# All weight chunks of a transformer block in fp32r high and low parts, and the modulation chunks moved behind attention's gates

## The chip, the core and the metric

One core of a Trainium2 chip runs the whole program as one launch. The metric is the device time in microseconds. Three runs of the kernel before took 2053.18, 2058.55 and 2112.91 us (median 2058.55 us).

## The reference, cut to what matters

Two blocks run one after the other on 256 tokens of 1024 channels. The first has two layers, and the change touches only these. Each layer is:

```python
h = rms_norm(x, norm_mix_pre[l])
proj = h @ w_in[l]            # q, k, v of three attentions, a small gate, conv and pooling inputs
...                           # compressed, selected and windowed attention; 31-tap conv; pooling
up = jnp.einsum("bsnc,ncd->bsnd", branches, w_branch[l])
gates = jax.nn.sigmoid((h @ w_gate[l]).reshape(bsz, seq, N_BRANCH, D_MODEL))
mix = jnp.einsum("bsnd,bsnd->bsd", gates, up) @ w_o[l]
x = x + rms_norm(mix, norm_mix_post[l])
hf = rms_norm(x, norm_ffn_pre[l])
u = causal_depthwise_conv(hf @ ffn_w_up[l], ffn_conv_w[l], ffn_conv_b[l])
gate, val = jnp.split(u, 2, axis=-1)
f = (jax.nn.gelu(gate, approximate=True) * val) @ ffn_w_down[l]
x = x + rms_norm(f, norm_ffn_post[l])
```

The second block (a state-space scan, attention and a mixture of experts) starts from six modulation vectors, `silu(c) @ w_mod + b_mod`. They don't depend on x. The kernel computes them inside the two layers of the first block, 24 steps of 128 columns in each layer, taken four at a time as six "mod steps".

## The kernel before, in words

**Weights come in chunks.** Every weight matrix is laid out in chunks of 128 partitions by 2048 float32 values, 1024 KB each, and TensorE works through them in one fixed order, 92 chunks in a layer. They pass through a ring of four slots, `ring`. SyncE loads chunk c + 4 into the slot of chunk c once TensorE has raised that slot's `used` semaphore (lines 398 to 402); the landed load raises the slot's `landed` semaphore. TensorE raises `used` of a chunk not at the chunk's last matmul but with the first matmul of the work behind it (`release` and `carry`, lines 419 to 428).

**Two forms of weights.** Some chunks are used as float32 straight from the ring: the projections (line 498), all `blocks_fm` chunks (line 526), the compression weights (line 555) and the modulation chunks (line 448). The others are split first, so that TensorE can use its fp32r form: ScalarE copies the chunk into a rounded high part (`split_hi`, line 386), VectorE subtracts that from the chunk and writes the low part (`split_lo`, line 392), and TensorE runs three matmuls, high by high, high by low and low by high. These are the branch projections (lines 717 to 721), `w_o` (736 to 740), the feed-forward's two matrices (759 to 763 and 777 to 781), and the experts of the second block. The activations of these matmuls are kept in two parts as well.

**Order of a layer's chunks:** two mod steps (4 chunks); key, value and query projections `kv`, `kv2`, `q`, `dq` (8 chunks); `c` and `ba` (2 + 2), four compression chunks, `bg` (2); 16 gate chunks with the four other mod steps laid between the first eight of them (a mod chunk, half a step, behind each); 12 branch and `w_o` chunks; 22 up and 11 down chunks of the feed-forward; one empty chunk.

**Orders of the engines.** Each engine executes its own instruction list strictly as it is written, and the lists are written by hand. What matters here is the attention stage. There are 12 attention items (kind, token tile t, head group g); items of t = 0 have 128 keys and those of t = 1 have 256. Turn i of the loop does on TensorE (lines 672 to 682): the scores of item i, one gate chunk with its mod chunk, the transposes of the probabilities of item i - 1 (`turn_probs`), and their product with the values (`values`, line 666). ScalarE's turn (lines 885 to 903): copy the gate result out of PSUM (`gate_out`), copy the mod row, copy the transposed probabilities of item i - 1 into `pt`, then the exponentials of item i. `values(i - 1)` waits for that `pt` copy. VectorE masks, takes maxima, normalizes, and runs ten steps of the 31-tap convolution in each turn. GpSimd has nothing to do in this stage. A fixed pool of PSUM regions is shared out by `Jobs`: a job claims its region when its last user is drained.

**The beginning of a layer:** ScalarE loads the column and row parameters (lines 801 and 802) and squares x; GpSimd takes the inverse root; VectorE waits for both parameter loads, scales x, and TensorE transposes it into `hT`. TensorE does the two early mod steps meanwhile.

Of the kernel before, what the change touches and what calls it, by code (L numbers as in the profile page):

```python
# [27 lines left out]
F32 = mybir.dt.float32  # L28
# [5 lines left out]
P = 128  # L34
T = 256
# [15 lines left out]
SPLITS = 3  # L51
FFN_CHUNKS = FB + FB // 2
# [5 lines left out]
def offsets(fields):  # L58
# [11 lines left out]
    ("w_ga", KD * 24),  # L70
])
ROWS, N_ROWS = offsets([("mix_post", D), ("ffn_post", D), ("sinks", 8)])
# [123 lines left out]
def plan_mods(jobs, steps):  # L196
    for i in steps:
        jobs.plan(("mod", i))
        if i - 1 in steps:
            jobs.plan(("modT", i - 1))  # L200


EARLY_MODS, MID_MODS = range(0, 2), range(2, MOD_STEPS)


def plan_layer(jobs):
    plan_mods(jobs, EARLY_MODS)
# [3 lines left out]
    jobs.plan(("modT", EARLY_MODS[-1]))  # L211
# [16 lines left out]
    for kv in range(2):  # L228
        jobs.plan(("hidT", kv), drains=2)
    jobs.plan(("bg", 1))  # L230
# [49 lines left out]
def layer_block(nc, l, mem, ring, landed, used, wts, psum, sems, cols_dram, rows_dram, loaded):  # L280
# [28 lines left out]
    lo_ready = sems("lo_ready")  # L309
# [9 lines left out]
    x, tm, hT, proj, gates, qTs, rkT = (mem[k] for k in ("x", "tm", "hT", "proj", "gates", "qTs", "rkT"))  # L319
# [3 lines left out]
    cdT = gates[:, 2048:3072].rearrange("p (m t) -> p m t", m=4)  # L323
    rtmp = gates[:, 3072:4480]
    rot = gates[:, 4480:7296].rearrange("p (t c) -> p t c", t=2)
    hfT, fT, split = (mem[k] for k in ("hfT", "fT", "split"))
# [2522 lines left out]
```

## Time and profile before

| what | us |
|---|---|
| runs of the kernel | 2053.18, 2058.55, 2112.91 |
| the profiled execution's own time | 2053.64 |
| its span in the trace | 2051.8 |
| layer 0 of the first block, about | 0 to 640 |
| layer 1, about | 640 to 1268 |
| TensorE busy | 1860.6 (91%) |
| VectorE busy | 953.2 (46%) |
| ScalarE busy | 647.4 (32%) |
| GpSimd busy | 217.5 (11%) |
| mean granted TensorE clock | 0.941 of full speed |

A time in the trace is counted from the start of the span. TensorE's busy time is that of overlapping matmuls, so the price of a chunk is read from start to start of the same instruction in two chunks, not from the mean duration of one. A float32 matmul stands in the trace as two matmul instructions, an fp32r one as one. An entry "x64" is 64 instructions of that line in a row; the bracket behind it says how long the engine stood idle before it and what ended the wait.

### The profile page before, as it was taken

The page shows a single profiled execution, that of the slowest core. Times are in us where ns is not written, and L with a number is a line of the kernel's source. Part 1 is how long each engine was busy: PE and PEld are TensorE (multiplying, and loading weights), DVE is VectorE, ACT ScalarE, POOL GpSimd, SP SyncE. Part 2 cuts the span into 40 slices and gives each one's busy share as a digit, 9 for nine tenths or more (in the row PEclk, how much of TensorE's full clock was granted, in tenths as well). Part 3 has the DMA queues.
Part 4 walks back from the last instruction along what each step waited for, and adds up shares of the span by engine and source line. Part 5 has one row for each costly group of instructions (what it writes and reads, how often), then busy time and mean ns, then how long its engine had stood idle before and what let it go on. Part 6 is the DMA issues. An engine that isn't in the chain of part 4 may idle for free. (4 is left out here: it accounts for less than half of the span.)

```text
span 2051.8 us, 24867 instructions
## 1 busy us (share of the span) xinstructions
PE 1860.6 (91%) x9940; PEld 1444.6 (70%) x9940; DVE 953.2 (46%) x1410; ACT 647.4 (32%) x987; POOL 217.5 (11%) x285
## 2 busy tenths in 40 slices
PE   6999998869996999998869997999899997899996
PEld 3577777869974477676859985544476645799995
DVE  1235464557742215454646743138434415355555
ACT  1122225445531112224545542111223401333331
POOL 0100000213310010000303320001520001000000
PEclk9999999989998999999989998899978997899998
DMA  7444422425455444522425545322110021355552
GB/s 275 143 185 164 185 84 102 152 106 182 180 182 219 163 184 145 204 85 80 154 97 182 185 168 188 123 82 82 41 42 1 1 103 62 106 183 189 179 183 82
DMA packets 39094, 279.81 MB, mean 136 GB/s; under 512 B 4432, under 2 KB 4688, under 8 KB 5840
## 3 DMA queue, kind: packets, MB, share of 16 engines
q1 hardware_dynamic: 37984, 272.44, 36.5%
q10 hardware_dynamic: 1008, 5.93, 0.8%
q8 instruction: 74, 1.21, 0.2%
q14 instruction: 28, 0.23, 0.0%
HBM read 277.30 MB, written 1.05 MB: 136 GB/s over the span
## 5 line engine op out<-in xcount | busy, mean ns | idle before, releaser
L526 PE MATMUL psum<-sb_hT,ring 128*128 128x256 f32 x1408 | 321.9, 388 | 2.2 <-DMA ring<-weights 2.1
L526 PEld LDWEIGHTS psum<-sb_hT,ring 128*128 128x128 f32 x1408 | 270.2, 194 | 49.1 <-issue 7.7
L392 DVE TENSOR_TENSOR sb_split<-ring,sb_split 128x2048 fp32r<-128x2048 f32 x90 | 212.4, 2360 | 123.7 <-ACT sb_split L386 123.4
L759 PE MATMUL psum<-sb_hfT,sb_split 128*128 128x256 f32 x704 | 201.4, 286 | 10.9 <-DVE sb_hfT L1279 10.9
L386 ACT ACTIVATE sb_split<-ring 128x2048 fp32r<-128x2048 f32 x90 | 171.9, 1910 | 114.9 <-PE psum L781 57.8
L762 PE MATMUL psum<-sb_hfT,sb_split 128*128 128x256 f32 x704 | 201.0, 286 | 0.0
L763 PE MATMUL psum<-sb_hfT,sb_split 128*128 128x256 f32 x704 | 200.9, 285 | 0.0
L1644 DVE TENSOR_TENSOR sb_split<-ring,sb_split 128x2048 fp32r<-128x2048 f32 x48 | 110.0, 2292 | 160.2 <-ACT sb_split L1639 160.2
L1937 PE MATMUL psum<-sb_hfS,sb_split 128*128 128x256 f32 x512 | 146.5, 286 | 2.5 <-PE psum L1959 2.1
L1940 PE MATMUL psum<-sb_hfS,sb_split 128*128 128x256 f32 x512 | 146.0, 285 | 0.0
L1941 PE MATMUL psum<-sb_hfS,sb_split 128*128 128x256 f32 x512 | 145.9, 285 | 0.0
L759 PEld LDWEIGHTS psum<-sb_hfT,sb_split 128*128 128x128 f32 x704 | 137.1, 195 | 11.4 <-DVE sb_hfT L1279 11.4
L762 PEld LDWEIGHTS psum<-sb_hfT,sb_split 128*128 128x128 f32 x704 | 137.1, 195 | 0.0
L763 PEld LDWEIGHTS psum<-sb_hfT,sb_split 128*128 128x128 f32 x704 | 137.0, 195 | 0.0
L1639 ACT ACTIVATE sb_split<-ring 128x2048 fp32r<-128x2048 f32 x48 | 91.6, 1908 | 95.8 <-PE psum L1898 47.0
L498 PE MATMUL psum<-ring,sb_hT 128*128 128x512 f32 x256 | 110.4, 593 | 0.0
L1937 PEld LDWEIGHTS psum<-sb_hfS,sb_split 128*128 128x128 f32 x512 | 99.4, 194 | 4.2 <-issue 3.8
L1309 DVE SCALAR_TENSOR_TENSOR sb_hq<-psum,sb_cols,sb_hq 128x254 f32<-128x254 f32 (+1 forms) x176 | 72.7, 475 | 61.8 <-ACT sb_hq L969 61.8
L1940 PEld LDWEIGHTS psum<-sb_hfS,sb_split 128*128 128x128 f32 x512 | 99.5, 194 | 0.3
L1941 PEld LDWEIGHTS psum<-sb_hfS,sb_split 128*128 128x128 f32 x512 | 99.4, 194 | 0.0
L1096 DVE SCALAR_TENSOR_TENSOR sb_acc<-sb_bglu,sb_cols,sb_acc 128x256 f32<-128x256 f32 x240 | 97.1, 476 | 0.0
L809 ACT ACTIVATE sb_gates<-psum 128x512 f32<-128x512 f32 x36 | 21.3, 597 | 232.7 <-PE psum L526 232.1
(352 smaller groups left out, 3221.2 us busy)
## 6 DMA issues: line engine op xcount, KB each, us to landing
ring<-weights SPq DMA_DIRECT2D x256, 1024.0 KB, 4.8
sb_rows<-rows ACTq DMA_DIRECT2D x2, 1028.0 KB, 10.6
sb_rows<-rows ACTq DMA_DIRECT2D x1, 2048.0 KB, 10.4
sb_cols<-cols ACTq DMA_DIRECT2D x2, 662.0 KB, 6.2
sb_x<-x_in SPq DMA_DIRECT2D x1, 1024.0 KB, 6.9
sb_y<-ctx_in SPq DMA_DIRECT2D x1, 1024.0 KB, 5.6
out<-sb_x SPq DMA_DIRECT2D x2, 512.0 KB, 2.7
sb_const<-const SPq DMA_DIRECT2D x1, 791.0 KB, 9.8
```

The costliest lines, as they stand in the source:

```text
L386: act.activation(slot[:, 0, :], ring[:, c % SLOTS, :], ACT.Copy).then_inc(hi_ready, 1)
L392: dve.tensor_tensor(slot[:, 1, :], ring[:, c % SLOTS, :], slot[:, 0, :].bitcast(F32), ALU.subtract).then_inc(lo_ready, 1)
L498: mm = pe.matmul(jobs.out((w, t)), hT[:, 4 * half + k, t * P:(t + 1) * P], chunk[:, k, :], start=(half == 0 and k == 0), stop=(half == 1 a ...
L526: mm = pe.matmul(jobs.out(name)[:, b * T:(b + 1) * T], chunk[:, k, b * P:(b + 1) * P], hT[:, k, :], start=(k == 0), stop=(k == KD - 1))
L759: mm = pe.matmul(out, hi[:, k, b * P:(b + 1) * P], hfT[:, 0, k, :], start=(k == 0), stop=False)
L762: pe.matmul(out, hi[:, k, b * P:(b + 1) * P], hfT[:, 1, k, :], start=False, stop=False)
L763: mm = pe.matmul(out, lo[:, k, b * P:(b + 1) * P], hfT[:, 0, k, :], start=False, stop=(k == KD - 1))
L1096: conv.up(dve.scalar_tensor_tensor(out=acc[:, b, :], in0=bglu[:, b, k:k + T], scalar=w, in1=acc[:, b, :], op0=ALU.mult, op1=ALU.add))
L1644: dve.tensor_tensor(split[:, n % SPLITS, 1, :], ring[:, (first_moe + n) % SLOTS, :], split[:, n % SPLITS, 0, :].bitcast(F32), ALU.subtract ...
L1937: mm = pe.matmul(out, hi[:, k, b * P:(b + 1) * P], hfS[:, 0, k, :], start=(k == 0), stop=False)
L1940: pe.matmul(out, hi[:, k, b * P:(b + 1) * P], hfS[:, 1, k, :], start=False, stop=False)
L1941: mm = pe.matmul(out, lo[:, k, b * P:(b + 1) * P], hfS[:, 0, k, :], start=False, stop=(k == KD - 1))
```

## The change

In each layer of the first block:

1. All weight chunks except the compression and modulation chunks are used in two parts: 30 more in a layer (8 projections, `c`, `ba`, `bg`, 16 gates). The normalized input is kept in two parts too (`hS`, in place of `hT`).
2. The low part is written where the chunk lay, in its ring slot (`ring_low` is the same memory as `ring`). High parts have two buffers up to the feed-forward (`HI_MIX`) and four in it (`HI_FFN`, before: three).
3. The low parts of gate chunks 0 to 12 are made by GpSimd, the others by VectorE.
4. All six mod steps lie behind the first twelve gate chunks; none is left at the start.
5. x and the constants are loaded ahead of the weights. The row parameters are loaded behind the projections, and those of the feed-forward later.
6. The small gate's product `ga` is computed turned round, four groups of 32 columns, and turned back by two matmuls.
7. The gates take other memory, and gate chunks run in the order of the branches that use them.

ScalarE's high parts are placed like this: those of the projections ahead of the copies of each pair; that of gate i + 2 right behind the copy of gate i.

```diff
+HI_MIX, HI_FFN = 2, 4
...
+MID_MODS = range(MOD_STEPS)
+
+def layer_chunks():
+    out = ["split"] * 12 + ["raw"] * 4 + ["split"] * 2
+    for i in range(16):
+        out.append("split")
+        if mid_mod_of(i) is not None:
+            out.append("raw")
+    return out + ["split"] * (12 + FFN_CHUNKS) + ["raw"]
+
+SPLIT_CHUNKS = [c for c, kind in enumerate(layer_chunks()) if kind == "split"]
+FIRST_C, FIRST_BA, FIRST_BG, FIRST_GATE, FIRST_UP, FIRST_WO, FIRST_FFN, FIRST_DOWN = 8, 10, 12, 14, 30, 38, 42, 64
+POOL_LOWS = range(FIRST_GATE, FIRST_GATE + 13)
...
     def split_hi(act, n):
 
-        c, slot, turns = split_slot(n)
-        if turns <= n < n_up or n >= n_up + turns:
-            act.wait_ge(used[(c - turns) % SLOTS], l * (N_LAYER_CHUNKS // SLOTS) + ((c - turns) // SLOTS + 1))
+        before = n - HI_MIX if n <= FIRST_FFN else n - HI_FFN if n >= FIRST_FFN + HI_FFN - 1 else -1
+        if before >= 0:
+            c = SPLIT_CHUNKS[before]
+            act.wait_ge(used[c % SLOTS], l * (N_LAYER_CHUNKS // SLOTS) + (c // SLOTS + 1))
+        c = SPLIT_CHUNKS[n]
         act.wait_ge(landed[c % SLOTS], (l * (N_LAYER_CHUNKS // SLOTS) + (c // SLOTS + 1)) * 16)
-        act.activation(slot[:, 0, :], ring[:, c % SLOTS, :], ACT.Copy).then_inc(hi_ready, 1)
+        act.activation(hi_of(n), ring[:, c % SLOTS, :], ACT.Copy).then_inc(hi_ready, 1)
...
@@ TensorE: one gate chunk in every turn @@
-                gate_chunks(i < len(ITEMS))
+                gate_chunks(1)
                 if i == 1:
                     cmp_out()
                 if i >= 1:
                     turn_probs(i - 1)
-                    gate_chunks(i in (3, 6))
                     values(i - 1)
             gate_chunks(16)
...
@@ ScalarE: gate_out @@
-                        copy_out(("gate", i), gates[:, i * 512:(i + 1) * 512])
+                        n = BRANCH_ORDER[i // 4]
+                        copy_out(("gate", i), gate_of[n][:, i % 4 * 512:(i % 4 + 1) * 512], func=ACT.Sigmoid if n == BRANCH_ORDER[-1] and i > 13 else ACT.Copy)
+                        split_hi(act, FIRST_GATE + i + 2)
                         if mid_mod_of(i) is not None and i % 2 == 1:
                             mods_out([mid_mod_of(i)])
...
@@ ScalarE, feed-forward loop @@
                 if j < FB:
-                    split_hi(act, n_up + j + SPLITS)
+                    split_hi(act, FIRST_FFN + j + HI_FFN)
...
@@ VectorE, behind the attention loop @@
+            split_lo(dve, FIRST_GATE + 13)
             out_low(len(ITEMS) - 1)
-            split_lo(dve, 0)
             conv_steps(4 * TAPS)
+            for n in range(FIRST_GATE + 14, FIRST_UP + 1):
+                split_lo(dve, n)
...
@@ GpSimd @@
+            for n in POOL_LOWS:
+                split_lo(pool, n)
+                pool.wait_ge(lo_pool, low_count(n))
...
@@ SyncE, start of the program @@
                     sp.dma_start(mem["cond"][:, :], cond).then_inc(conditioned, 16)
+                    sp.dma_start(mem["x"][:, :, :], x_in.rearrange("(t p) d -> p t d", p=P)).then_inc(loaded, 16)
+                    sp.dma_start(mem["const"][:, :], const).then_inc(placed, 16)
                     for s in range(SLOTS):
                         sp.dma_start(ring[:, s, :], weights[s]).then_inc(landed[s], 16)
```

## Rows read from the trace of the kernel before

**Rows 1.** The page, part 1: busy time and share of the span

```profile
PE 1860.6 (91%) x9940; PEld 1444.6 (70%) x9940; DVE 953.2 (46%) x1410; ACT 647.4 (32%) x987; POOL 217.5 (11%) x285
```

**Rows 2.** TensorE timeline, one turn: start, busy, instruction, count, [idle before]

```profile
192.88 1.06 PE L448 MATMUL psum<-ring,sb_cvec 128*32 128x512 f32 x8
...
195.24 1.07 PE L666 MATMUL psum<-sb_pt,sb_proj 128*64 128x512 f32 x2 [0.70 <-ACT sb_pt L809]
...
197.33 7.17 PE L526 MATMUL psum<-sb_hT,ring 128*128 128x256 f32 x32
...
204.43 1.06 PE L448 MATMUL psum<-ring,sb_cvec 128*32 128x512 f32 x8
```

**Rows 3.** Timeline of ScalarE, the same turn

```profile
194.10 0.60 ACT L809 ACTIVATE sb_mrow<-psum 128x512 f32<-128x512 f32 x1 [0.51 <-PE psum L448]
...
194.59 0.59 ACT L809 ACTIVATE sb_pt<-psum 128x512 f32<-128x512 f32 x1
```

**Rows 4.** Timeline of the load queue, the same turn

```profile
194.21 0.86 SPq L402 DMA_DIRECT2D ring<-weights  x2
```

**Rows 5.** Source view of the loads, line 402, 150 to 240 us

```profile
DMA to landing us min/median/max: 4.7/5.7/8.0
```

**Rows 6.** Timeline of TensorE, a turn with 256 keys

```profile
282.53 1.93 PE L666 MATMUL psum<-sb_pt,sb_proj 128*64 128x512 f32 x4
...
284.39 1.99 PE L640 MATMUL psum<-sb_rkT,sb_qTs 64*128 64x256 f32 x8
```

**Rows 7.** Timeline of ScalarE, the same turn

```profile
281.30 0.59 ACT L809 ACTIVATE sb_pt<-psum 128x512 f32<-128x512 f32 x1
...
282.64 0.60 ACT L809 ACTIVATE sb_pt<-psum 128x512 f32<-128x512 f32 x1 [0.75 <-PE psum L435]
```

**Rows 8.** Timeline of TensorE, weights as whole float32

```profile
31.02 55.18 PE L498 MATMUL psum<-ring,sb_hT 128*128 128x512 f32 x128
...
90.43 13.98 PE L526 MATMUL psum<-sb_hT,ring 128*128 128x256 f32 x64
```

**Rows 9.** Timeline of ScalarE, one chunk to the next, both part forms

```profile
458.34 1.02 ACT L969 ACTIVATE sb_hq<-psum,sb_cols 128x256 f32<-128x256 f32 x2 [1.21 <-PE psum L763]
...
464.10 1.02 ACT L969 ACTIVATE sb_hq<-psum,sb_cols 128x256 f32<-128x256 f32 x2 [2.63 <-PE psum L763]
...
592.63 1.92 ACT L386 ACTIVATE sb_split<-ring 128x2048 fp32r<-128x2048 f32 x1 [3.52 <-PE psum L781]
...
598.07 1.92 ACT L386 ACTIVATE sb_split<-ring 128x2048 fp32r<-128x2048 f32 x1 [3.52 <-PE psum L781]
```

**Rows 10.** Timeline of VectorE, one low part

```profile
573.02 2.29 DVE L392 TENSOR_TENSOR sb_split<-ring,sb_split 128x2048 fp32r<-128x2048 f32 x1 [2.54 <-ACT sb_split L386]
```

**Rows 11.** Source view of GpSimd line 2586: ns least, median, most

```profile
L2586 POOL TENSOR_TENSOR sb_wx<-sb_xs,sb_sm x6: 1899/1900/2236, 1457.3 to 1474.7; 128x1024 f32<-128x1024 f32 x6
```

**Rows 12.** Windows: busy PE, PEld, DVE, ACT, POOL; granted clock, DMA share, GB/s

```profile
322.60:325.10 2.50, 0.01 (x1) 0.00 (x0) 1.56 (x3) 0.84 (x4) 0.00 (x0) 1.00 0.32 134
...
327.30:330.50 3.20, 3.20 (x4) 0.54 (x3) 0.00 (x0) 0.49 (x1) 0.00 (x0) 0.50 0.00 0
```

**Rows 13.** Timeline of TensorE, first and last gate of layer 0

```profile
153.04 8.83 PE L526 MATMUL psum<-sb_hT,ring 128*128 128x256 f32 x32
...
330.65 7.17 PE L526 MATMUL psum<-sb_hT,ring 128*128 128x256 f32 x32
```

**Rows 14.** Timeline of TensorE between the projections and attention, layer 0

```profile
125.42 1.68 PE L555 MATMUL psum<-ring,sb_gates 128*32 128x256 f32 x16 [2.94 <-DMA ring<-weights]
...
127.90 9.46 PE L526 MATMUL psum<-sb_hT,ring 128*128 128x256 f32 x32 [0.81 <-DMA ring<-weights]
```

**Rows 15.** Timeline of VectorE, start of layer 1

```profile
653.30 1.42 DVE L992 TENSOR_SCALAR sb_tm<-sb_x,sb_small 128x1024 f32<-128x1024 f32 x2 [13.24 <-DMA sb_rows<-rows]
```

**Rows 16.** Timeline of TensorE, first projection of layer 1

```profile
658.60 41.88 PE L498 MATMUL psum<-ring,sb_hT 128*128 128x512 f32 x97
```

**Rows 17.** The page, part 5: busy, mean ns | idle before, what ended it

```profile
L777 PE MATMUL psum<-sb_split,sb_fT 128*128 128x512 f32 x176 | 70.0, 398 | 5.6 <-DVE sb_hq L1309 5.6
```

More of the change, by code:

```diff
@@ L193, in mid_turn_of, with low_count @@
     return MID_MODS[i // 2 - 1] if i % 2 == 0 and 1 <= i // 2 <= len(MID_MODS) else None
[L196 to L203, printed above, removed]
+MID_MODS = range(MOD_STEPS)
[9 more added lines that the diff above has]
+POOL_LOWS = range(FIRST_GATE, FIRST_GATE + 13)
+def low_count(n):
+    return sum((m in POOL_LOWS) == (n in POOL_LOWS) for m in range(n + 1))
 def plan_layer(jobs):
-    plan_mods(jobs, EARLY_MODS)
     for c in range(2):
@@ L277, with layer_block @@
 BRANCH_ORDER = (2, 0, 3, 1)
-def layer_block(nc, l, mem, ring, landed, used, wts, psum, sems, cols_dram, rows_dram, loaded):
+def layer_block(nc, l, mem, ring, ring_low, landed, used, wts, psum, sems, cols_dram, rows_dram, loaded, placed):
     filled = {r: sems(f"filled_{r}") for r in REGION}
@@ L511, in _ @@
             jobs.claim(pe, "ga")
[L512 removed]
+            for part in range(2):
                 for k in range(KD):
[L514 to L516 removed]
+                    mm = pe.matmul(jobs.out("ga")[32 * (k % 4):32 * (k % 4) + 32, 0:T], C("w_ga", 32 * k, 32 * k + 32),
+                                   hS[:, part, k, :].bitcast(F32), start=(part == 0 and k < 4), stop=(part == 1 and k >= 4))
+                    if part == 0 and k == 0:
                         carry(mm)
@@ L572, in _ @@
                 jobs.fill(mm, ("hidT", kv))
+            jobs.wait_drained(pe, "ga")
+            jobs.claim(pe, "gaT")
+            for t in range(TT):
+                mm = pe.matmul(jobs.out("gaT")[:, 24 * t:24 * t + 24], gaT[:, t * P:(t + 1) * P], K("sel", 0, 24), start=True, stop=True)
+            jobs.fill(mm, "gaT")
             release(blocks_fm(("bg", 1)))
@@ L726, in _ @@
                 for half in range(2):
-                    hi, lo = (part.rearrange("p (k n) -> p k n", k=4) for part in next_split(8 + 2 * c + half))
+                    hi, lo = (part.rearrange("p (k n) -> p k n", k=4) for part in next_split())
                     for i in range(2):
@@ L1231, in _ @@
                     jobs.wait_filled(dve, name)
-                    g2 = gates[:, n * 2048 + i * 512:n * 2048 + (i + 1) * 512]
+                    g2 = gate_of[n][:, i * 512:(i + 1) * 512]
+                    if n == BRANCH_ORDER[-1] and i >= 2:
+                        jobs.wait_drained(dve, ("gate", 12 + i))
                     if bi == 0:
@@ L1254, in _, with residual @@
                                   ALU.subtract).then_inc(mix_lo, 1)
-            for n in range(9, n_up):
+            for n in range(FIRST_WO + 1, FIRST_FFN + 1):
                 split_lo(dve, n)
-            def residual(kind, g, first):
+            def residual(kind, first):
                 for t in range(TT):
@@ L2652, in place @@
                     mem1[k] = stack.enter_context(nc.sbuf_tensor(f"sb_{k}", [P, *s], dtype))
+            place(first, MEM_HI)
             with ExitStack() as phase:
@@ L2656, in build_program @@
             place(first, MEM_BR1)
+            with ExitStack() as phase:
+                place(phase, MEM_ROT)
             with ExitStack() as phase:
@@ L2661, in build_program @@
                 place(phase, MEM_UP)
-            for fields, dtype in ((MEM_FFN_SPLIT, F32R), (MEM_FFN, F32)):
-                for k, s in fields.items():
-                    mem1[k] = first.enter_context(nc.sbuf_tensor(f"sb_{k}", [P, *s], dtype))
+            place(first, MEM_FFN)
             with nc.Block() as block:
@@ L2700, in build_program @@
             with nc.Fori(0, LAYERS) as l:
-                layer_block(nc, l, mem1, ring, landed, used, weights, psum, sems, cols, rows, loaded)
+                layer_block(nc, l, mem1, ring, ring_low, landed, used, weights, psum, sems, cols, rows, loaded, placed)
                 nums = [s.num for s in layer_sems]
```

351 lines of the change are left out of this document (188 added, 163 removed).

## The prediction

> **What bounds the kernel now.** The page first: TensorE is busy for 91% of the span and no other engine for half of it [rows 1]. So a microsecond off TensorE's list is worth one, unless another engine's list then ends later. Next the TensorE timeline over one turn of layer 0's attention [rows 2]. From the mod chunk at 192.88 to the next at 204.43 are 11.55 us, 7.10 of them the gate chunk, and only 0.70 idle, waiting for ScalarE's copy of the probabilities. ScalarE has made that copy by 195.18 because nothing stands before it in its list but two short copies [rows 3]. Last the load queue: the slots of the gate chunk and the mod chunk just used are refilled from 194.21 on, 1.33 us after 192.88 [rows 4], and a load lands 4.7 us after its issue at the least, 5.7 in the median [rows 5]. Today the next chunk but one can't be wanted before 204.43, where TensorE leaves the gate between; the load is hidden. The change alters exactly this.
>
> **What TensorE gains.** A float32 chunk costs 55.18 / 8 = 6.90 us with 512 columns and 13.98 / 2 = 6.99 us with 256 [rows 8]. In parts the same chunk takes 598.07 - 592.63 = 5.44 us (24 matmuls of 512) and 464.10 - 458.34 = 5.76 us (48 of 256) [rows 9], 0.120 us for each of the latter. Per layer: 8 projections x 1.46 = 11.7 us; c and ba 4 x 1.23 = 4.9; the turned small gate about 1.6 (32 narrow matmuls in four column groups, nearest the compression chunks' form in [rows 14]: 1.68 us for 16 with the clock low). The Trainium skill, TensorE: Matmul & The Clock Gate, "Wait — 56ns, not 53.3ns?", gives the start-to-start time as columns by clock plus 2.5 ns, so 0.109 us at 256. By that a chunk would take 5.24 us and the 44 chunks of this width in both layers 23 us less than in my sum; the trace's 0.120 us is the measurement and I keep it.
>
> **Feeding the projections** costs nothing in a steady stream: from a chunk's release, 1.92 us for the high part and 2.29 for the low [rows 9, 10] and about 0.3 between them are 4.5, less than 5.44. The cover is thin (0.9 us). Between c and ba it tears: ScalarE puts a high part before the copies that free PSUM regions for ba, which I price at one high part, 2.0. At the compression chunks TensorE already waits 2.94 and 0.81 us for loads [rows 14]; now bg waits for high and low part behind the landing, +4.4, against two cheaper chunks (-2.5) and some small work (-0.4): +1.5. One more high part stands before the rotated queries' copies: +1.2. Projections to the first gate, per layer: -11.7 - 4.9 - 1.6 + 2.0 + 1.5 + 1.2 = -13.5; two layers -27.0.
>
> **The attention turn.** ScalarE now makes the high part of gate i + 2 directly behind the copy of gate i. In a layer the gates and mod chunks alternate up to gate 11, two chunks in a turn, four slots: chunk gate i + 2 goes into the very slot that gate i has just left. So ScalarE waits for a whole load. Queued behind it are the mod row's copy, the pt copy and the exponentials; `values(i - 1)` waits for the pt copy, and behind `values` on TensorE stand the next scores and the next gate. From the start of the mod chunk: 1.33 to the issue [rows 4], 4.7 to landing [rows 5], 1.91 high part, 0.60 pt copy [rows 3], 0.06, then 2.09 from `values` to the next gate's start [rows 2], 5.76 for the gate. That is 16.45 us against 11.55. The mod chunk, its turning and the transposes hide in the wait. A turn with an odd gate copies a mod row first, +0.5 [rows 3].
>
> **The clock.** In this turn TensorE idles some 5 to 6 us. In [rows 12] an idle stretch of 2.5 us is followed by 3.2 us at half the granted clock (1.2 for 2.4 GHz) while TensorE is busy all the time: 1.6 us lost. I charge 1.6 for each such wait; 0 and, from the same row stretched over the values, scores and gate of the turn, 7.85 are the ends.
>
> **The stage added up,** from the first gate's start. Gate 0: 5.76 + 1.6 = 7.4. To the end of gate 1, no probabilities yet: 7.85. Gate 2, behind the compressed attention's copy, which also waits: 6.03 + 1.91 + 0.5 + 0.6 + 5.76 + 1.6 = 16.4. Gates 3 to 6: 4 x (16.45 + 1.6) + 1.0 = 73.2. Gates 7 and 8, scores over 256 keys (+0.85, 1.99 against 1.16 to 1.2) [rows 6]: 38.3. Gates 9 to 11, also a second transpose and copy (+1.34 [rows 7]) and longer values (+0.86 [rows 6]): 3 x 21.1 + 0.5 = 63.8. Gate 12, whose successor's load is no longer late: 16.3. Gate 13 waits for a low part that VectorE makes only behind the last weighing: 18.0. Gates 14 and 15, again behind VectorE's low parts: 23.3. Sum 264.5 us. Today it is from 153.04 to 337.66, 184.6 us [rows 13]. So +79.9 a layer, +159.8 in all.
>
> GpSimd's low parts cost nothing here: 1.90 us for 1024 columns [rows 11] make 3.8 for 2048, bounded by 1.9 (a fixed cost only) and 7.6 (twice, beside a busy VectorE), and each has a turn of 16 us and a gate's lead. Their cover would last even at the old pitch of 11.55. VectorE's and ScalarE's added work in the turns (1.91 us of ScalarE) lies in waits.
>
> **The rest.** At the program's start x and the constants land earlier, and row parameters hold nobody; the first projection moves from 31.0 to about 19, behind a chain of about 7.2 us from the scaled x (three scalings, parts, then one low part of 2.29): -12.0. In layer 1 VectorE no longer waits for rows until 653.30 [rows 15] but starts at 650, so the two high-low chains take what was saved and the projection starts at 658.5 as now [rows 16], on a low clock: +1.6. In the feed-forward four high buffers make the same pattern, chunk j + 4 waits for the slot of chunk j, but it only delays ScalarE by 2 us in a turn of 5.76 and TensorE leads on; at its end TensorE waits longer for the last drain, today 5.6 / 2 = 2.8 us [rows 17], by 3.6 to 5: +8.0 in all, between 0 and 10. The second buffer filled earlier ahead of the branches: -2.8. The row and feed-forward parameter loads are three queue entries on ScalarE of some 0.5 us each, in waits.
>
> **Sum:** 2053.6 (the profiled execution's own time) - 27.0 + 159.8 - 12.0 + 1.6 + 8.0 - 2.8 = 2181.2, so 2181 us. That execution is 5 us below the median shown, 2058.55.
>
> **Rivals.** (1) *The load is no wait*, the forecast's opposite: if ScalarE found the chunk landed, the turn would be TensorE's alone. It decides at a landing within about 1.7 us of the release, where TensorE's own mod chunk and transposes end. Then the stage gives 32 x 1.23 = -39.4 and pays 11.8 for four more mod halves and two turnings per layer: 2053.6 - 27.0 - 39.4 + 11.8 - 12.0 + 1.6 + 8.0 - 2.8 = 1994. For it: TensorE idles little now and the copy waits of 0.7 are small. Against it: no load in the stretch landed in under 4.7 us, and the slot arithmetic leaves no lead. A misreading of mine somewhere in the order is what I give it its chance for: 0.13. (2) *The clock stays low* from one turn to the next, as each gate is followed by a longer idle time than any gate has now: 11 turns x 6.25 x 2 = +137, 2318 us: 0.04. For it: both idle stretches of [rows 14] together had a gate chunk at 9.46. Against: in [rows 13] 8.83 us is the worst that a low clock did to one gate without them. (3) *Half the wait*: TensorE or the queue has a lead of 3 us that I don't see; 22 turns x 3.0 and half of the clock's price are -66 - 22: 2093, around the 2% line, 0.07. The forecast has 0.76. The Trainium skill, DMA: Bandwidth & Descriptors, "Rules for kernel authors", says to issue a load early and wait late; the change waits as early as it can, and the 4.7 us row is why that would hurt.
>
> **Range and chances.** Within the forecast: without the clock's price (28 waits x 1.6) 2136, with landing at the median of 5.7 in all 22 waits 2203, with the clock's price doubled 2226, both together 2248. To reach 8 in 10 the range goes down through the half wait: 2085 to 2245. I count as no change what lies within 2% (41 us), about what a measurement of this kernel can tell. Faster 0.13; same 0.06; slower 0.81.
>
> **What would show it.** In the changed kernel's trace ScalarE's high-part line must stand under "DMA ring<-weights" as releaser for over 100 us in total (11 waits of about 5.4 in each layer), and the TensorE line of the values product must show idle time behind ScalarE's pt copy of 4 to 6 us a turn in place of 0.7. Start to start of gate chunks 16 to 22 us; projections 5.44 a chunk; first projection near 19 us; granted clock below 0.90 in the attention windows. The prediction is wrong if the pitch of turns stays under 12 us, if the pt copy isn't what `values` waits for, or if the high parts wait for GpSimd's or VectorE's low parts instead of the load.

## The result, and the profile after

The changed kernel takes 2240.47 us, the median of 4 runs (2239.11 to 2243.20); the kernel before, on the same chip, 2059.22 (4 runs). One of those four, 2112.91 us, fell into a slower state of the chip, and the ratio leaves it out: 1.089, 95% interval 1.087 to 1.092, so 181 us or 9% slower. I had forecast 2181 us in a range of 2085 to 2245: the direction and the mechanism are right, the size is 59 us short, and the measured time lies 5 us inside the top of the range.

The profiled execution spans 2237.3 us where before it was 2051.8. Its page, parts 1, 2 and 5 (the columns are those of [rows 1, 17]):

```profile
PE 1869.7 (84%) x10780; PEld 1507.6 (67%) x10780; DVE 1047.0 (47%) x1452; ACT 754.9 (34%) x1055; POOL 382.2 (17%) x311
...
PEclk9987778898999898777889899979987999789998
...
L404 ACT ACTIVATE sb_hi<-ring 128x2048 fp32r<-128x2048 f32 x118 | 225.7, 1912 | 404.2 <-DMA ring<-weights 251.8
...
L410 POOL TENSOR_TENSOR ring_low<-ring,sb_hi 128x2048 fp32r<-128x2048 f32 x26 | 119.9, 4610 | 426.0 <-ACT sb_hi L404 426.0
```

TensorE falls from 91% to 84% of a longer span, and its clock stands at 0.7 or 0.8 through both attention stages (slices 3 to 8 and 16 to 21 of 55.9 us). ScalarE's high part waits 251.8 us for loads; 58.1 of them, in 11 waits, lie in layer 0's stage of gates and as many in layer 1's, the others at loads elsewhere. Who waits for ScalarE shows in the waits of TensorE (total us, times, longest):

```profile
PE psum L690 <- ACT sb_pt L822: 78.8, 12, 7.5
...
PE psum L454 <- ACT sb_pt L822: 52.1, 12, 7.5
...
PE psum L454 <- ACT sb_cpT L822: 15.0, 2, 7.5
```

`values` and the second transposes waited 0.7 us a turn [rows 2]; now it is up to 7.5, and 145.9 us in all with the compressed attention's copy. One turn of layer 0, which answers to [rows 2]; the timeline of TensorE (start, duration, line, idle time before it and what ended it):

```profile
194.66 1.07 PE L467 MATMUL psum<-ring,sb_cvec 128*32 128x512 f32 x8
195.65 0.65 PE L454 MATMUL psum<-sb_const,sb_sc 128*128 128x128 f32 x4
203.60 1.97 PE L690 MATMUL psum<-sb_pt,sb_proj 128*64 128x512 f32 x2 [7.29 <-ACT sb_pt L822]
205.50 2.07 PE L664 MATMUL psum<-sb_rkT,sb_qTs 64*128 64x128 f32 x8
207.50 0.58 PE L545 MATMUL psum<-sb_hS,sb_hi 128*128 128x256 f32 x1
```

ScalarE in the same turn, answering to [rows 3]:

```profile
194.76 0.60 ACT L822 ACTIVATE sb_tm<-psum 128x512 f32<-128x512 f32 x1 [10.33 <-PE psum L549]
200.67 1.91 ACT L404 ACTIVATE sb_hi<-ring 128x2048 fp32r<-128x2048 f32 x1 [5.31 <-DMA ring<-weights]
202.48 0.58 ACT L822 ACTIVATE sb_mrow<-psum 128x512 f32<-128x512 f32 x1
202.96 0.59 ACT L822 ACTIVATE sb_pt<-psum 128x512 f32<-128x512 f32 x1
```

and the load queue, answering to [rows 4]:

```profile
195.98 0.86 SPq L421 DMA_DIRECT2D ring<-weights  x2
```

So: modulation chunk at 194.66, issue 1.32 us later, landed 4.69 after that, high part 1.91, mod row, pt copy, and `values` at 203.60. What follows runs at half clock. The same turn in windows (us; busy us and count of each engine; granted clock; share and GB/s of the DMA engines):

```profile
196.30:200.30 4.00, 0.01 (x1) 0.00 (x0) 0.00 (x0) 0.00 (x0) 0.00 (x0) 1.00 0.79 295
...
202.00:203.60 1.60, 0.00 (x0) 0.00 (x0) 0.00 (x0) 1.60 (x4) 0.88 (x1) 0.50 0.33 138
203.60:207.50 3.90, 3.90 (x10) 2.06 (x10) 0.00 (x0) 1.48 (x8) 3.63 (x1) 0.50 0.01 4
207.50:211.80 4.30, 4.30 (x21) 4.30 (x21) 4.02 (x10) 0.00 (x0) 0.00 (x0) 0.51 0.00 0
211.80:215.20 3.40, 3.40 (x30) 3.29 (x28) 2.26 (x6) 0.00 (x0) 0.00 (x0) 1.00 0.00 0
```

Where the 185.5 us of the span lie, from the starts of TensorE's groups in both traces (layer 0 / layer 1):

| stretch | before | after | measured | forecast |
|---|---|---|---|---|
| start to the first projection | 31.0 | 20.2 | -10.8 | -12.0 |
| eight projections | 55.0 / 55.0 | 46.5 / 47.1 | -16.4 | -23.4 |
| small gate to gate 0 | 67.0 / 67.2 | 75.1 / 75.7 | +16.6 | -3.6 |
| gate 0 to the end of gate 15 | 184.6 / 184.6 | 280.4 / 280.6 | +191.8 | +159.8 |
| branches and output projection | 92.4 / 92.3 | 90.9 / 90.7 | -3.1 | -2.8 |
| feed-forward | 200.6 / 203.5 | 205.2 / 204.7 | +5.9 | +8.0 |
| change of layers | 27.9 | 27.5 | -0.5 | +1.6 |
| the rest | 790.5 | 792.6 | +2.1 | 0 |
| sum | | | +185.6 | +127.6 |

Two stretches hold 52 of the 58 us between measured and forecast: 32 us in attention, 20 us ahead of it. The rest is the second block, which no edit here touches. From the same matmul of that block to the end the twelve traces take 699.3 to 703.6 us, so a difference of 4 us between two times can lie there; where a few microseconds matter, the experiments below are read by stretches.

### The profile page after: what moved, and what is told of

Its sections match the earlier page's. It is cut to its first block and busy times, and to the rows that moved or that the text cites. A ratio compares the mean times of both kernels' runs of the same rounds, so it can differ in the third digit from the quotient of the medians.

```text
span 2237.3 us, 26793 instructions
## 1 busy us (share of the span) xinstructions
PE 1869.7 (84%) x10780; PEld 1507.6 (67%) x10780; DVE 1047.0 (47%) x1452; ACT 754.9 (34%) x1055; POOL 382.2 (17%) x311
## 5 line engine op out<-in xcount | busy, mean ns | idle before, releaser
L404 ACT ACTIVATE sb_hi<-ring 128x2048 fp32r<-128x2048 f32 x118 | 225.7, 1912 | 404.2 <-DMA ring<-weights 251.8
L410 DVE TENSOR_TENSOR ring_low<-ring,sb_hi 128x2048 fp32r<-128x2048 f32 x92 | 211.7, 2303 | 231.6 <-ACT sb_hi L404 231.6
L545 PE MATMUL psum<-sb_hS,sb_hi 128*128 128x256 f32 x704 | 225.0, 320 | 40.3 <-DVE ring_low L410 25.2
L548 PE MATMUL psum<-sb_hS,sb_hi 128*128 128x256 f32 x704 | 218.6, 310 | 0.0
L549 PE MATMUL psum<-sb_hS,ring_low 128*128 128x256 f32 x704 | 216.9, 308 | 0.0
L777 PE MATMUL psum<-sb_hfT,ring_low 128*128 128x256 f32 x704 | 198.0, 281 | 0.0
L545 PEld LDWEIGHTS psum<-sb_hS,sb_hi 128*128 128x128 f32 x704 | 155.8, 221 | 55.5 <-DVE ring_low L410 32.1
L1701 DVE TENSOR_TENSOR sb_split<-ring,sb_split 128x2048 fp32r<-128x2048 f32 x48 | 110.0, 2292 | 160.1 <-ACT sb_split L1696 160.1
L548 PEld LDWEIGHTS psum<-sb_hS,sb_hi 128*128 128x128 f32 x704 | 155.6, 221 | 0.0
L549 PEld LDWEIGHTS psum<-sb_hS,ring_low 128*128 128x128 f32 x704 | 155.5, 221 | 0.0
L1696 ACT ACTIVATE sb_split<-ring 128x2048 fp32r<-128x2048 f32 x48 | 91.6, 1908 | 94.3 <-PE psum L1955 47.0
L1994 PEld LDWEIGHTS psum<-sb_hfS,sb_split 128*128 128x128 f32 x512 | 99.2, 194 | 4.1 <-issue 3.8
```

Source lines behind the costliest of these rows:

```text
L404: act.activation(hi_of(n), ring[:, c % SLOTS, :], ACT.Copy).then_inc(hi_ready, 1)
L410: eng.tensor_tensor(low_of(n), ring[:, SPLIT_CHUNKS[n] % SLOTS, :], hi_of(n).bitcast(F32), ALU.subtract)\
L545: mm = pe.matmul(out, hi[:, k, bs], hS[:, 0, k, :], start=(k == 0), stop=False)
L548: pe.matmul(out, hi[:, k, bs], hS[:, 1, k, :], start=False, stop=False)
L549: mm = pe.matmul(out, lo[:, k, bs], hS[:, 0, k, :], start=False, stop=(k == KD - 1))
L777: mm = pe.matmul(out, lo[:, k, b * P:(b + 1) * P], hfT[:, 0, k, :], start=False, stop=(k == KD - 1))
```

## Experiments

**1. The high part behind the exponentials** (changed kernel, one step moved):

```diff
+            later = []
+
+            def late_parts():
+                while later:
+                    split_hi(act, later.pop(0))
...
-                        split_hi(act, FIRST_GATE + i + 2)
+                        later.append(FIRST_GATE + i + 2)
...
                 if i < len(ITEMS):
                     exps(i)
+                late_parts()
```

> The changed kernel, with one thing moved: in the attention loop ScalarE makes the high part of gate i + 2 behind the exponentials of the turn, not directly behind the copy of gate i. The same work, the same loads, the same two high buffers. Theory of the prediction (ScalarE's wait for a whole load stands in front of the pt copy): nothing of the turn is queued behind that wait any more, TensorE sets the turn again at 10 to 10.6 us (11.55 before, less 1.3 for the gate chunk in parts), the stage from the first gate to the end of gate 15 falls from 280.6 us to 170 to 180, and the time from 2240 to about 2030 (2015 to 2050). Rival A (the loss comes from the modulation chunks in every turn, or from GpSimd's low parts, and not from where ScalarE waits): the stage stays above 250 us, the time above 2180. Rival B (half of it each): 2100 to 2150.

Measured: 2067.15 us (9 runs), ratio to before 1.006 (1.0044 to 1.0076). 173 of the 181 us are gone. The even turns are 10.3 us (gate chunks at 203.59 and 213.88 in layer 0), and the pt copy is waited for by 0.70 us again. ScalarE still waits for loads, 246.6 us in the whole program for 337.0 (both kinds of high part counted) and 13.1 for 58.1 in layer 0's stage, but with nothing behind the wait that TensorE wants in that turn. The stage is 197.5 us, not 170 to 180, and the time lies 37 us above what I expected and outside the range of 2015 to 2050. TensorE's and ScalarE's timelines, then VectorE's and GpSimd's:

```profile
180.86 0.58 PE L545 MATMUL psum<-sb_hS,sb_hi 128*128 128x256 f32 x1 [5.68 <-POOL ring_low L410]
...
203.59 0.38 PE L545 MATMUL psum<-sb_hS,sb_hi 128*128 128x256 f32 x1
...
211.79 1.07 PE L690 MATMUL psum<-sb_pt,sb_proj 128*64 128x512 f32 x2 [0.70 <-ACT sb_pt L822]
...
213.88 0.38 PE L545 MATMUL psum<-sb_hS,sb_hi 128*128 128x256 f32 x1
...
215.62 1.92 ACT L404 ACTIVATE sb_hi<-ring 128x2048 fp32r<-128x2048 f32 x1 [2.26 <-DMA ring<-weights]
...
206.69 8.38 DVE L1165 SCALAR_TENSOR_TENSOR sb_acc<-sb_bglu,sb_cols,sb_acc 128x256 f32<-128x256 f32 x10
...
206.50 4.73 POOL L410 TENSOR_TENSOR ring_low<-ring,sb_hi 128x2048 fp32r<-128x2048 f32 x1 [5.85 <-ACT sb_hi L404]
```

Gates 2 and 3 wait 2.7 and 5.7 us for GpSimd's low part, gates 13 and 14 wait 4.8 and 4.0 for VectorE's. And ten filter steps of VectorE, 4.04 us elsewhere, last 8.38 beside a low part of 4.73. The wait behind the gate's copy is shown as the cause; a second cost comes up, on GpSimd.

**2. The high part between pt copies and exponentials** (against experiment 1):

```diff
+                late_parts()
                 if i < len(ITEMS):
                     exps(i)
-                late_parts()
```

> As late_hi, but the high part of gate i + 2 stands between the pt copies and the exponentials of the turn. ScalarE still waits for the load in mid turn, only the waiter differs: values no longer hang on it, the exponentials do. Worked out for the turns over 128 keys: 1.3 + 4.7 + 1.9 from the modulation chunk's start to the high part's end, 1.6 for four exponentials, 1.1 for the weighing make 10.6 us, where TensorE comes to the next transposes after 11.3: covered. Over 256 keys about 2.0 and 1.8: 11.7, 0.4 to 1 us a turn short in five turns. Theory of the prediction (what costs is values behind the pt copy): 2030 to 2050, at most 20 us behind late_hi. Rival (any wait of ScalarE for a load within the turn costs about its length): above 2130.

Measured: 2095.35 us (4 runs), ratio 1.017 (1.011 to 1.024), 28 us behind experiment 1: neither the 20 of the theory nor the rival's 2130. VectorE, GpSimd and TensorE in a turn:

```profile
198.26 2.96 DVE L1237 TENSOR_TENSOR sb_small<-sb_small 128x4 f32<-128x4 f32 x1
...
196.62 4.57 POOL L410 TENSOR_TENSOR ring_low<-ring,sb_hi 128x2048 fp32r<-128x2048 f32 x1 [11.45 <-ACT sb_hi L404]
...
202.00 1.00 PE L454 MATMUL psum<-sb_const,sb_sc 128*128 128x128 f32 x4 [1.22 <-DVE sb_sc L1240]
```

A product over four columns, 0.16 us elsewhere, lasts 2.96 and ends with GpSimd's low part at 201.2. The weighing is late by that, TensorE waits 1.22 us, and the next gate begins on half clock (8.06 us for 5.92). That the late weighing comes from GpSimd is so far read from the times alone; experiment 10 tests it.

**3. TensorE kept busy in the wait** (transposes repeated; the waits stay):

```diff
+WARM = 10
...
-                    mm = pe.transpose(out[0:n, i * P:(i + 1) * P], b, ident)
+                    mm = pe.transpose(out[0:n, i % 4 * P:(i % 4 + 1) * P], b, ident)
...
-                    transpose4(("PT", a, t, g, kb), [sc[:, i % 2, j, kb * P:(kb + 1) * P] for j in range(4)])
+                    blocks = [sc[:, i % 2, j, kb * P:(kb + 1) * P] for j in range(4)]
+                    transpose4(("PT", a, t, g, kb), blocks * (WARM if kb == 0 and i < 11 else 1))
```

> The changed kernel with the waits left in and TensorE kept busy in them: the four transposes of the probabilities are made ten times over (about 6 us in a wait of 6 to 7.4 us), in the 11 turns whose gate is followed by a load. The outputs are the same. What the granted clock costs is measured by this. Theory 1 (the forecast's price of 1.6 us for each wait): 22 waits give back 35, 2205. Theory 2 (read from the changed kernel's trace: values, scores and the first 4.3 us of the gate run at half clock after each wait, 0.9 + 0.9 + 2.1 = 3.9 us): turns fall from 20.7 to about 16.8 us, 22 of them give back 84, about 2155 (2140 to 2175). Theory 3 (the slow matmuls are not the clock, or repeated transposes don't keep it): 2240 to 2245.

Measured: 2219.13 us (4 runs), ratio 1.081 (1.075 to 1.086): above theory 1's 2205 and below theory 3's 2240, so none of the three came out. A transpose at full clock takes 0.116 us, so the filling was too short. The windows from the end of a wait of 3.57 us on, and from the end of the next, 2.10 us:

```profile
199.64:202.36 2.72, 2.72 (x11) 1.69 (x11) 0.00 (x0) 1.47 (x8) 2.72 (x1) 0.75 0.00 0
202.36:207.00 4.64, 4.64 (x22) 4.64 (x22) 4.36 (x11) 0.00 (x0) 0.91 (x1) 0.50 0.00 0
...
219.22:221.30 2.08, 2.08 (x10) 1.16 (x10) 0.00 (x0) 1.48 (x8) 2.08 (x1) 1.00 0.00 0
221.30:227.10 5.80, 5.80 (x49) 5.72 (x48) 5.41 (x14) 0.00 (x0) 2.08 (x1) 1.00 0.00 0
```

The clock held behind waits of 1.19 and 2.10 us and fell behind those of 3.57 and 3.47, but in this trace it fell behind one of 2.31 as well (0.67 from 258.06 to 260.90, then 0.50). The expectation of experiment 4 calls the first of these 4.5 us, with the last transposes counted in, and leaves out the wait of 2.31.

**4. The same with the wait filled:**

```diff
-WARM = 10
+WARM = 13
...
-                    transpose4(("PT", a, t, g, kb), blocks * (WARM if kb == 0 and i < 11 else 1))
+                    transpose4(("PT", a, t, g, kb), blocks * (WARM + 3 * (i % 2) if kb == 0 and i < 11 else 1))
```

> As warm_turns, with more of the repeated transposes: sixteen times where no row of modulations is turned, thirteen times where one is. At full clock a transpose took 0.116 us, so ten rounds filled only 4.6 us and left gaps of 2.1 to 4.5 us; in that kernel the clock held over gaps of 1.2 and 2.1 us and fell in those of 3.5 and 4.5. Now 7.4 and 6.0 us are filled. Theory (the granted clock falls only where TensorE stands idle, and the low clock adds 3.5 to 4 us to a turn over 128 keys and about 1.5 to one over 256 keys): all gates of these turns take 5.9 us, turns come every 16.6 to 17.3 us, 6 or 7 turns of 3.6 and 4 of 1.5 us in each layer give back 60 us: 2175 to 2190. Rival (the clock falls for another reason): near 2219, as warm_turns.

Measured: 2190.64 us (4 runs), ratio 1.066 (1.062 to 1.069), 0.6 us above the theory's range of 2175 to 2190. The windows from the product with the values on:

```profile
202.00:204.10 2.10, 2.06 (x10) 1.16 (x10) 0.00 (x0) 1.52 (x8) 2.10 (x1) 1.00 0.00 0
204.10:208.00 3.90, 3.90 (x33) 3.87 (x33) 3.59 (x9) 0.00 (x0) 1.62 (x1) 1.00 0.02 4
```

Gates 3 to 7 start at 187.24, 204.13, 220.56, 237.48 and 254.79: every 16.4 to 17.3 us, against 20.3 to 21.9 in the changed kernel. From gate 2 to gate 11 it is 161.6 us against 190.9: the half clock costs 29.3 us over nine turns, 3.3 a turn: 3.8 to 4.7 in the six from gate 3 to gate 9, 1.5 to 1.7 in the other three. The repeated transposes cost 7 us a layer in the two last turns that have them, where no load is late. So of 59 us some 45 are left, which is what the two layers are shorter by; the other 3.5 of the 48.8 us between the two spans lie in the second block.

**5. The low parts of gates 0 and 1 on VectorE:**

```diff
-POOL_LOWS = range(FIRST_GATE, FIRST_GATE + 13)
+POOL_LOWS = range(FIRST_GATE + 2, FIRST_GATE + 13)
...
+            split_lo(dve, FIRST_GATE)
...
                     cmp_weigh()
+                    split_lo(dve, FIRST_GATE + 1)
```

> The changed kernel with the low parts of gates 0 and 1 on VectorE in place of GpSimd. In the changed kernel's trace VectorE's gating product ahead of gate 0 lasts 3.27 us and the first four filter steps 5.59 us where they took 0.69 and 1.37 before, and both lie beside a low part on GpSimd. Theory (the two engines get in each other's way): 0.69 and 1.37 us again, the first gate starts about 3.5 to 4.5 us earlier in each layer, the time falls by 6 to 9 us. Rival (the length comes from somewhere else, such as the data's place): the durations stay, VectorE has 4.6 us more in its list and the time rises by 0 to 5 us.

Measured: 2225.20 us (4 runs), ratio 1.083 (1.079 to 1.087), 15 us faster than the changed kernel (14.1 by the spans) where I expected 6 to 9. The low part of gate 0 now stands ahead of bg's gating product. VectorE, GpSimd and gate 0 in the changed kernel:

```profile
121.66 3.27 DVE L1139 TENSOR_TENSOR sb_bglu<-sb_bglu,sb_sc 128x512 f32<-128x512 f32 x1 [2.28 <-ACT sb_sc L822]
132.13 5.59 DVE L1154 TENSOR_SCALAR sb_acc<-sb_bglu,sb_cols 128x256 f32<-128x256 f32 x4
...
119.86 4.53 POOL L410 TENSOR_TENSOR ring_low<-ring,sb_hi 128x2048 fp32r<-128x2048 f32 x1 [36.57 <-ACT sb_hi L404]
132.95 4.62 POOL L410 TENSOR_TENSOR ring_low<-ring,sb_hi 128x2048 fp32r<-128x2048 f32 x1 [8.57 <-ACT sb_hi L404]
...
141.82 0.55 PE L545 MATMUL psum<-sb_hS,sb_hi 128*128 128x256 f32 x1 [3.69 <-DVE sb_brS L1174]
```

and with the low parts moved:

```profile
121.65 0.68 DVE L1140 TENSOR_TENSOR sb_bglu<-sb_bglu,sb_sc 128x512 f32<-128x512 f32 x1
...
131.76 1.37 DVE L1155 TENSOR_SCALAR sb_acc<-sb_bglu,sb_cols 128x256 f32<-128x256 f32 x4
...
137.69 0.38 PE L545 MATMUL psum<-sb_hS,sb_hi 128*128 128x256 f32 x1
```

The durations are again those of before. Gate 0 starts 4.1 us earlier with no wait, and at full clock (its first matmul 0.38 us, not 0.55), so it also ends 2.2 sooner; I had left the clock out of this expectation too. That the two engines hold each other up is said by the Trainium skill too, SBUF — State Buffer, "Who interferes with whom": a VectorE instruction with both inputs in SBUF, or in a two-port mode, and a GpSimd instruction that reads SBUF lock each other out for a whole instruction. The trace agrees for two inputs, with 3.27 for 0.69 us and 2.96 for 0.16. The third, 5.59 for 1.37, has one input tensor; whether it ran in a two-port mode the trace doesn't show. It is the rule that I should have weighed against "GpSimd's low parts cost nothing here".

**6. The feed-forward's high part one step later:**

```diff
                 if j >= 1:
+                    split_hi(act, FIRST_FFN + j - 1 + HI_FFN)
...
-                if j < FB:
-                    split_hi(act, FIRST_FFN + j + HI_FFN)
```

> The changed kernel with the feed-forward's high part of chunk j + 3 made behind the first filter step of j, in place of chunk j + 4 behind the activation of j - 1, and VectorE's low part one step later too. TensorE waits 6.8 and 5.6 us ahead of the down projection in the changed kernel, where it waited 2.8 before. Theory of the prediction (ScalarE's wait for the slot just left delays the last drains): the wait goes back to about 2.8 or less and the time falls by 7 to 10 us, 2231. Rival (it is the GpSimd product, 1.65 us a chunk where it took 0.82, that is late): the wait stays at 5 us or more.

Measured: 2233.20 us (4 runs), ratio 1.086 (1.083 to 1.089), 7.3 us faster than the changed kernel (6.7 by the spans). The down projection's first matmul in the changed kernel and in this one:

```profile
655.11 0.77 PE L791 MATMUL psum<-sb_hi_ffn,sb_fT 128*128 128x512 f32 x1 [6.79 <-issue]
```

```profile
651.45 0.47 PE L791 MATMUL psum<-sb_hi_ffn,sb_fT 128*128 128x512 f32 x1 [2.85 <-issue]
```

2.8 us, as before [rows 17]. The rival falls too: GpSimd's product became slower still, 2.48 us in the mean for 1.65, and the long wait is gone all the same. The page, part 5:

```profile
L1450 POOL TENSOR_TENSOR sb_cpad<-sb_hq 128x256 f32<-128x256 f32 x44 | 109.1, 2480 | 135.6 <-ACT sb_hq L1007 135.6
```

**7. The modulation chunks alone** (kernel before, float32 chunks; with them comes the change's one gate chunk in every turn):

```diff
-EARLY_MODS, MID_MODS = range(0, 2), range(2, MOD_STEPS)
+EARLY_MODS, MID_MODS = range(0, 0), range(MOD_STEPS)
...
-                gate_chunks(i < len(ITEMS))
+                gate_chunks(1)
...
-                    gate_chunks(i in (3, 6))
...
-                turned = {1: 0, 3: 1, 4: 2, 6: 3}
+                turned = {1: 0, 3: 1, 5: 2, 7: 3, 9: 4, 11: 5}
```

> The kernel before with one part of the change alone: all six modulation steps of a layer stand behind gate chunks (one half behind each of gates 0 to 11), none ahead of the projections; chunks stay float32, x and the row parameters are loaded as before. Theory of the prediction (the loss needs a high part that waits for the slot just left; a float32 chunk is wanted only a whole turn later): no more than the moved work itself, 2 steps of 3 us a layer moved from where they were partly hidden, 2050 to 2068. Rival A (the alternation of gates and modulation chunks in every turn costs by itself): 20 us or more above before, over 2077.

Measured: 2052.00 us (10 runs), ratio 0.9977 (0.9956 to 0.9999), within the 2050 to 2068 expected. Its TensorE, one turn:

```profile
202.97 7.17 PE L523 MATMUL psum<-sb_hT,ring 128*128 128x256 f32 x32
...
212.43 1.07 PE L663 MATMUL psum<-sb_pt,sb_proj 128*64 128x512 f32 x2 [0.71 <-ACT sb_pt L805]
...
214.52 1.78 PE L523 MATMUL psum<-sb_hT,ring 128*128 128x256 f32 x7
```

11.55 us, 0.71 idle, as in [rows 2]. Gates and modulation chunks in turn, with the same slots, cost 1.8 us of the stage (186.5 for 184.6). The loss needs the high part in ScalarE's list. The first projection starts at 23.3 us here: 7.7 of the 10.8 us won at the start are there as soon as the modulation chunks have left it; what loading x first would give by itself no run shows.

**8. The orders mended together** (experiments 1, 5 and 6; gate 3's high part ahead of gate 2's copy; bg's sigmoid ahead of gate 0's high part; low parts of gates 13 to 15 on GpSimd):

```diff
-POOL_LOWS = range(FIRST_GATE, FIRST_GATE + 13)
+POOL_LOWS = range(FIRST_GATE + 2, FIRST_GATE + 16)
...
-            split_hi(act, FIRST_GATE)
             copy_out(("bg", 0), sg[:, 0, :], func=ACT.Sigmoid)
+            split_hi(act, FIRST_GATE)
```

> The changed kernel with the four orders mended together: high parts of gates behind the exponentials (as late_hi; that of gate 3 ahead of gate 2's copy), low parts of gates 0 and 1 on VectorE and those of gates 13 to 15 on GpSimd, bg's sigmoid ahead of gate 0's high part, the feed-forward's order of ffn_order. From late_hi's 2067: gates 0 and 1 -15 (as front_low), sigmoid -3, feed-forward -9, the waits of 4.8 and 4.0 us ahead of gates 13 and 14 -17, half of those ahead of gates 2 and 3 -8: about 2015 (2005 to 2035), 1 to 2.5% faster than before. Rival (something else is late in their place, above all GpSimd with 4.6 us for each low part): 2045 to 2065.

Measured: 2009.52 us (5 runs), ratio 0.977 (0.975 to 0.979), as expected (2005 to 2035). Gates 13 and 14 no longer wait; gate 2 still does, 2.4 us for GpSimd.

**9. All low parts on VectorE:**

```diff
-POOL_LOWS = range(FIRST_GATE + 2, FIRST_GATE + 16)
+POOL_LOWS = range(0)
...
                 if i >= 1:
                     weigh(i - 1)
+                    split_lo(dve, FIRST_GATE + (2 if i == 1 else i + 2))
```

> As all_mended, with every low part on VectorE and none on GpSimd: 2.29 us in place of 4.6 each, that of gate i + 2 behind the weighing of turn i. Theory (a low part on GpSimd costs twice: 4.6 us until TensorE may start, and VectorE's instructions with two inputs in memory held up beside it): gate 2's wait of 2.4 us and the half clock behind it go (3.7), four waits of 0.7 us for the weighing too (2.8), both in each layer: 2009.5 - 13, about 1997 (1990 to 2005). Rival (VectorE becomes what sets the turn: 3.4 for mask and weighing, 2.3 low part, 4.0 filter, 0.2 are 9.9 us of the 10.3 to 11.2 that TensorE takes, and more over 256 keys): 2010 to 2030.

Measured: 1988.32 us (5 runs), ratio 0.967 (0.966 to 0.969): 69 us or 3.3% faster than before, 252 faster than the changed kernel, with the same arithmetic, and 9 us below what I expected, just under the range of 1990 to 2005. Page and waits of TensorE:

```profile
PE 1777.1 (89%) x10780; PEld 1443.9 (73%) x10780; DVE 1089.6 (55%) x1478; ACT 756.4 (38%) x1055; POOL 298.8 (15%) x285
...
PE psum L454 <- ACT sb_pt L822: 8.4, 12, 0.7
PE psum L690 <- ACT sb_pt L822: 7.1, 10, 0.8
```

Of the 145.9 us of waits behind ScalarE's copies about 17 are left (0.74 a layer for the compressed attention's copy); the first gate to the end of gate 15 is 166.7 us (137.21 to 303.90). VectorE's low part takes 2.28 us and the ten filter steps behind it 4.05:

```profile
189.29 2.28 DVE L410 TENSOR_TENSOR ring_low<-ring,sb_hi 128x2048 fp32r<-128x2048 f32 x1
191.49 4.05 DVE L1167 SCALAR_TENSOR_TENSOR sb_acc<-sb_bglu,sb_cols,sb_acc 128x256 f32<-128x256 f32 x10
```

**10. Experiment 9 with the high part ahead of the exponentials:**

```diff
+                late_parts()
                 if i < len(ITEMS):
                     exps(i)
-                late_parts()
```

> As all_vector, with the high part of gate i + 2 between the pt copies and the exponentials, as in mid_hi. mid_hi was 28 us slower than late_hi where I expected at most 20, and in its trace a product over 4 columns on VectorE lasted 2.96 us (0.16 elsewhere) beside a low part on GpSimd; the weighing came late and TensorE's clock fell. Theory (the shortfall of mid_hi beyond what its wait costs comes from GpSimd): without GpSimd's low parts 2 to 15 us above all_vector. Rival (it is ScalarE's wait in mid turn itself, GpSimd only happens to be there): again 25 to 40 us above all_vector.

Measured: 2000.73 us (5 runs), ratio 0.973 (0.971 to 0.974), 12.4 us above experiment 9, within the theory's 2 to 15, where with GpSimd's low parts it was 28.2. The traces of layer 0 show where each lies. From gate 3 to gate 12 this kernel takes 107.9 us and experiment 9 the same; with GpSimd's low parts it was 124.7 in experiment 2 against 113.0 in experiment 1. So in these turns ScalarE's wait costs nothing by itself, and what it cost came through GpSimd. What is left comes from one place in each layer: ScalarE's wait in turn 0 makes the first exponentials late, the weighing and VectorE's low part of gate 2 behind them too, and gate 2 waits 1.82 us and takes 8.66 in place of 5.92. From gate 0 to gate 3 are 32.9 us for 27.5, which makes 10.7 us in two layers; the other 3.9 of the 14.6 us between the two spans lie in the second block. (Between the pairs lie the other orders of experiment 8 too; the low parts of gates 13 to 15 and the feed-forward are outside these turns.)

```profile
154.16 0.58 PE L545 MATMUL psum<-sb_hS,sb_hi 128*128 128x256 f32 x1 [1.82 <-DVE ring_low L410]
```

## Why the prediction was right in kind and short in size

**The attention turn: right, nearly to the tenth.** The forecast chained 1.33 + 4.7 + 1.91 + 0.60 + 0.06 + 2.09 + 5.76 = 16.45 us, 16.95 with a mod row. With the clock held up (experiment 4) turns come every 16.43 and 16.89 to 16.92. Taking that one wait out of the way of the pt copy gives back 173 us (experiment 1). The stage by gates, from the end of the gate before to the end of its own, layer 0: gate 0 8.1 (forecast 7.4), gate 1 7.9 (7.85), gate 2 16.6 (16.4), gates 3 to 6 81.9 (73.2), 7 and 8 43.9 (38.3), 9 to 11 63.3 (63.8), 12 15.9 (16.3), 13 19.2 (18.0), 14 and 15 23.7 (23.3). Gates 3 to 8 hold 14.3 of the 15.9 us by which the stage is longer than forecast.

**The clock's price: the step that failed.** "I charge 1.6 for each such wait; 0 and ... 7.85 are the ends." Measured 3.3 a turn, 3.8 to 4.7 from gate 3 to gate 9. The 1.6 came from a stretch [rows 12] in which TensorE was at work again as the clock fell. Here the clock is at half already at 202.0, the wait ends at 203.6, and values, scores and the first 4.3 us of the gate lie in it; all dense matmuls, which take twice the time. The bound of 7.85 was right, the choice near its lower end was not: a stretch behind a wait of 7.3 us was read from one behind a wait of 2.5. That is 15 us a layer. In three of the nine turns (from gate 2, 9 and 10 on) the charge was right, 1.5 to 1.7 us.

**GpSimd's low parts "cost nothing here": the second step that failed.** The duration, 4.6 us, lay between the bounds (1.9 and 7.6), 0.8 above my 3.8. In the changed kernel's own turns it hides, as the wait is longer. Ahead of gate 0 it holds up VectorE (experiment 5: 15 us in both layers with the clock that follows), and once the turns are short it is the next wait (experiments 1, 8 and 9). "Their cover would last even at the old pitch" held from gate 4 on, where no gate waits for a low part in experiment 1 until gate 13, and not for gates 2 and 3, which wait 2.7 and 5.7 us.

**Small gate to gate 0: -1.8 a layer forecast, +8.3 measured.** The stall between c and ba is 1.5 us (2.0 forecast). From ba to bg are 24.0 us for 22.1, as forecast (4.4 for the longer wait, 2.5 off for ba's two chunks). Left out was what ScalarE's high part of gate 0 stands in front of: bg's sigmoid, for which the second bg chunk waits 3.9 us. With the sigmoid first it waits 2.1 (experiment 8), and on low clock the chunk takes 8.0 us. The rest is VectorE, above.

**Projections: -8.2 a layer, forecast -11.7.** At full clock a chunk takes 24 x 0.232 = 5.6, not 5.44, and the first matmuls behind a wait of 5.5 us run at half clock, about 2 us. The Trainium skill's start-to-start time (TensorE: Matmul & The Clock Gate, "Wait — 56ns, not 53.3ns?"), by which I weighed 5.24 us for a chunk over 256 columns, isn't reached here: from gate 1's start to the next instruction are 5.85 us at full clock. Keeping the trace's 5.76 was right.

**The feed-forward's end** waits 6.8 and 5.6 us for 2.8, forecast 3.6 to 5 us more; experiment 6 shows the cause. The start (-10.8 for -12.0), the branches (-3.1 for -2.8) and the change of layers (-0.5 for +1.6) are as forecast within 2 us, though experiment 7 puts most of the start down to the modulation chunks.

**The rivals.** The load is no wait: refuted by the 11 waits for loads in each layer's stage, 58.1 us (5.3 each, where the forecast had 5.4), and by experiment 1. Half the wait: refuted, the issue to landing is 4.69 us of 4.7. The clock stays low from turn to turn: not quite, each gate ends at full clock (the window from 211.8), but this rival's direction was the right one; between it and the forecast lies the result. The chunk of 9.46 us that it leans on [rows 14] is the first bg chunk, not a gate.

**The range held partly by luck.** Its top of 2248, cut to 2245, was added up from a landing one microsecond later in 22 waits (22 us) and the clock's price doubled (45 us). The landing came as forecast, the clock took some 30 us more, and 20 us came from the stretch between the small gate and gate 0, for which the range had no term.

## What to carry to other kernels

A step that waits for a load is priced by what stands behind it in the same engine's list, not by its own 1.9 us: moved behind the last thing that the bounding engine wants in that turn, the same step with the same loads gave back 173 of 181 us. Price a wait of the matmul engine with the clock that it comes back to, over everything dense that follows, and take that from a wait as long as the one forecast. Before work goes to GpSimd "because it is idle", list what VectorE does with two inputs in memory in the same microseconds.

## What was not expected of the hardware

- Subtracting over 2048 columns took 4.6 us on GpSimd and 2.29 on VectorE; 1024 columns had taken GpSimd 1.9 [rows 11], so twice the columns took 2.4 times as long. The Trainium skill, GPSIMD Engine Reference, "3.1 Elementwise — side-by-side cycle accounting", gives 4497 and 2293 ns for an addition of this size; the trace agrees, with 4.50 to 4.7 where nothing held it up and 2.29. My 3.8, doubled from the shorter row, was the poorer source.
- The two engines' hold on each other runs both ways. GpSimd's feed-forward product rose from 0.82 to 1.65 us in the mean (44 times, off the path). In the row below it starts at 645.34, beside a low part of VectorE from 644.09 to 646.38, and ends 0.6 us after that:

```profile
644.09 2.29 DVE L410 TENSOR_TENSOR ring_low<-ring,sb_hi 128x2048 fp32r<-128x2048 f32 x1 [1.72 <-ACT sb_hi L404]
...
645.34 1.63 POOL L1448 TENSOR_TENSOR sb_cpad<-sb_hq 128x256 f32<-128x256 f32 x1 [2.66 <-ACT sb_hq L1005]
```

- Why a projection's matmul starts every 0.232 us where the feed-forward's of the same width took 0.227 [rows 9] stays open; no run here separates it.
